# A hybrid decoder layer on one core: the two up-projections as two passes of split products, in place of one pass in full precision

## The reference

```
ga = sigmoid(proj[..., OFF_GATE:OFF_GATE + D_MODEL])
gb = sigmoid(proj[..., OFF_GATE + D_MODEL:N_IN])
m = ga * (o_fox @ w_up_fox) + gb * (o_gdn @ w_up_gdn)     # w_up_*: 1024 x 2048
x = x + m @ w_out                                         # w_out: 2048 x 2048
```

## Time and profile before

| | us |
|---|---|
| runs | 3332.43, 3326.76, 3321.94 |
| median | 3326.76 |
| profiled execution, time | 3323.48 |
| profiled execution, span in the trace | 3321.8 |
| mean granted TensorE clock, share of full | 0.942 |

### The profile page before, as it was taken

The page is one execution under the profiler, slowest core; times in us unless marked ns, Lnnn a source line. Parts: engine busy times, 40 slices in busy tenths (PEclk is TensorE's granted clock), DMA queues, the critical chain, the costliest instruction groups (busy, mean ns, idle before and its releaser), DMA issues.

```text
span 3321.8 us, 62255 instructions
## 1 busy us (share of the span) xinstructions
PE 2974.1 (90%) x23103; PEld 2821.5 (85%) x23103; DVE 1966.2 (59%) x3901; ACT 1291.2 (39%) x2225; POOL 187.6 (6%) x203
## 2 busy tenths in 40 slices
PE   6999899787888997706999999999899999999989
PEld 6999689566666897705999999999789999999979
DVE  4467467332332255597666666666766666666654
ACT  4455420032231044303544444444444444444444
POOL 0000110000000000005100000000520000000000
PEclk8999889589899998858999999999999999999999
DMA  5554200267676453200455554455034455455533
GB/s 186 184 182 178 106 1 1 82 254 285 250 287 234 152 190 120 96 0 0 149 181 177 180 185 177 178 184 183 26 136 181 177 180 185 178 178 183 183 143 128
DMA packets 82018, 519.70 MB, mean 156 GB/s; under 512 B 9186, under 2 KB 9458, under 8 KB 28914
## 3 DMA queue, kind: packets, MB, share of 16 engines
q1 hardware_dynamic: 69394, 468.37, 39.0%
q0 software_dynamic: 11360, 45.61, 3.6%
q10 hardware_dynamic: 1152, 4.19, 0.3%
HBM read 508.75 MB, written 9.39 MB: 156 GB/s over the span
## 4 chain that ended last, share of the span: by engine, by line
PE 79%; DMA 7%; DVE 7%; POOL 2%; issue 2%; SPq 2%; POOLq 0%; ACT 0%; DVEq 0%; ACTq 0%
PE ps L563 22%; PE ps L564 22%; PE ps L565 21%; PE ps L943 4%; DMA arena<-in_vx 3%; DMA arena<-in_kx 3%; PE ps L1006 2%; POOL arena L1363 2%; PE ps L744 2%; SPq L477 1%; PE ps L623 1%; DVE arena L1907 1%; PE ps L732 1%; PE ps L558 1%; PE ps L615 1%
## 5 line engine op out<-in xcount | busy, mean ns | idle before, releaser
L563 PE MATMUL ps<-split 128*128 128x264 f32 x6288 | 1807.1, 287 | 52.1 <-DVE split L405 52.1
L564 PE MATMUL ps<-split 128*128 128x264 f32 x6288 | 1797.3, 286 | 0.0
L565 PE MATMUL ps<-split 128*128 128x264 f32 x6288 | 1791.8, 285 | 0.0
L405 DVE TENSOR_TENSOR split<-arena,split 128x512 fp32r<-128x512 f32 x1568 | 1079.8, 691 | 920.9 <-ACT split L400 918.1
L400 ACT ACTIVATE split<-arena 128x512 fp32r<-128x512 f32 x1568 | 987.7, 632 | 1340.1 <-PE ps L565 1339.7
L563 PEld LDWEIGHTS ps<-split 128*128 128x128 f32 x6288 | 1196.6, 190 | 81.9 <-issue 45.6
L564 PEld LDWEIGHTS ps<-split 128*128 128x128 f32 x6288 | 1196.5, 190 | 1.3 <-issue 0.5
L565 PEld LDWEIGHTS ps<-split 128*128 128x128 f32 x6288 | 1191.8, 190 | 0.3
L1952 DVE TENSOR_TENSOR arena<-arena,ps 128x264 f32<-128x264 f32 x512 | 216.5, 423 | 5.9 <-PE ps L565 5.9
L1363 POOL TENSOR_TENSOR arena<-arena 128x512 f32<-128x512 f32 x66 | 121.7, 1844 | 1264.1 <-DVE arena L1907 1264.1
L1006 PE MATMUL ps<-arena 128*128 128x128 f32 x1056 | 136.3, 281 | 40.5 <-POOL arena L1363 40.5
(11 more groups left out here) (302 smaller groups left out, 1572.6 us busy)
## 6 DMA issues: line engine op xcount, KB each, us to landing
arena<-in_wd SPq DMA_DIRECT2D x280, 1024.0 KB, 4.8
arena<-in_vd SPq DMA_DIRECT2D x128, 1024.0 KB, 4.8
arena<-in_kx POOLq DMA_DIRECT2D x32, 512.0 KB, 7.0
arena<-in_kx SPq DMA_DIRECT2D x32, 512.0 KB, 4.3
arena<-in_vx SPq DMA_DIRECT2D x32, 512.0 KB, 3.9
arena<-in_vx POOLq DMA_DIRECT2D x32, 512.0 KB, 7.2
arena<-in_state POOLq DMA_DIRECT2D x8, 512.0 KB, 7.4
o_ss<-arena ACTq DMA_DIRECT2D x8, 512.0 KB, 8.0
```

Source lines behind the costliest of these rows:

```text
L405: nc.vector.tensor_tensor(ckl(q), at(WR + (s % 4) * D_MODEL + q * QW, QW), as_f32(ckh(q)), ALU.subtract).then_inc(lo_ready, 1)
L563: mm(out, wh, xh, start=start, stop=False)
L564: mm(out, wh, xl, start=False, stop=False)
L565: return mm(out, wl, xh, start=False, stop=stop)
```

## The change

The up-projections join the split stream, in two passes of 8 units. A unit now holds the 8 input blocks of one branch for two output blocks. The first pass, `upg`, is the GDN branch, and stands ahead of `sot`; the second, `upf`, the attention branch, behind it. Each pass needs the high and low part of its 8 activation blocks, one copy of 2112 columns on ScalarE (`oh_split`) and one subtraction of 2112 columns on VectorE (`ol_split`) for each. `upg`'s results are multiplied into the gates in place (`gate_gdn`); `upf`'s are multiplied, added to these and split (`merge`). The merged blocks lie in two places (`MH`, `ML`), and `out` reads them there. The ring's slots are now given back by `lo_ready` in every stage; x is loaded again after `upg`, since it waits for `of_ready`.

```diff
-            ("gates0", 16), ("spt", 2), ("spb", 1), ("gates1", 16), ("sot", 1), ("up", 16), ("out", 16),
+            ("gates0", 16), ("spt", 2), ("spb", 1), ("gates1", 16), ("upg", 16), ("sot", 1), ("upf", 16), ("out", 16),
...
+        MH, ML = (HH + 8 * T, AH), (HL + 8 * T, AL)
...
+            def up_pass(name, s0, xh, xl):
+                with pe.Fori(0, 2) as it:
+                    for j in range(RING):
+                        for q in range(RING):
+                            n = JOB[name] + 2 * j + q // 2
+                            if q % 2 == 0:
+                                pe.wait_ge(evac[n % 4], it * 2 + n // 4)
+                            wait_low_part(pe, it, 4, s0 + j, q)
+                            for kk in range(QK):
+                                k = (q % 2) * QK + kk
+                                last = products(bank(n)[:, 0:T], ckh(q)[:, kk * P:(kk + 1) * P], ckl(q)[:, kk * P:(kk + 1) * P],
+                                                xh(k), xl(k), k == 0, k == NH - 1)
+                            last.then_inc(quarter_done, 1)
+
+            pe.wait_ge(ol_split, 1)
+            up_pass("upg", S0["up"], lambda k: sp_(AH + k * T, T), lambda k: sp_(AL + k * T, T))
+
             n = JOB["sot"]
...
-            pe.wait_ge(of_ready, 1)
-            with pe.Fori(0, 4) as it:
-                for j in range(RING):
-                    n = JOB["up"] + j
-                    pe.wait_ge(w_loaded[j], it * 16 + 16 * (S0["up"] // 4 + 1))
-                    pe.wait_ge(evac[n % 4], it + n // 4)
-                    for half in range(2):
-                        for k in range(NH):
-                            last = mm(ps[:, n % 4 + 4 * half, 0:T], wr(j)[:, (half * NH + k) * P:(half * NH + k + 1) * P],
-                                      ot3[:, half * NH + k, :], start=(k == 0), stop=(k == NH - 1))
-                    last.then_inc(pe_job, 1)
+            pe.wait_ge(ol_split, 2)
+            up_pass("upf", S0["up"] + 8, lambda k: hh3[:, k, :], lambda k: hl3[:, k, :])
             pe.wait_ge(mt_ready, 1)
...
+            act.wait_ge(bn_ready, 40)
+            A(sp_(AH, NH * T), at(OT + NH * T, NH * T), ACT.Copy).then_inc(oh_split, 1)
+            dense_steps(act, S0["up"], 2, high_part, lambda it, j: None, True, False)
+            act.wait_ge(of_ready, 1)
+            A(sp_(HH, NH * T), at(OT, NH * T), ACT.Copy).then_inc(oh_split, 1)
...
+            dense_steps(act, S0["up"] + 8, 2, high_part, merged_high, False)
...
+            dve.wait_ge(oh_split, 1)
+            V.tensor_tensor(sp_(AL, NH * T), at(OT + NH * T, NH * T), as_f32(sp_(AH, NH * T)), ALU.subtract).then_inc(ol_split, 1)
...
+            def merge(it, j):
+                for i in range(2):
+                    n, b = JOB["upf"] + 2 * j + i, 2 * j + i
+                    wait_quarter(dve, it, 4, S0["up"] + 8 + j, 2 * i + 1)
+                    m, t = at(TMU + i * 2 * T, T), at(TMU + (i * 2 + 1) * T, T)
+                    V.tensor_tensor(t, up_block(GT, it, b), bank(n)[:, 0:T], ALU.mult).then_inc(evac[n % 4], 1)
+                    dve.wait_ge(evac[n % 4], it * 2 + (n // 4 + 1))
+                    V.tensor_tensor(m, t, up_block(GT + 16 * T, it, b), ALU.add).then_inc(merged, 1)
+                for i in range(2):
+                    b = 2 * j + i
+                    dve.wait_ge(merged, it * 8 + (b + 1))
+                    dve.wait_ge(mh_ready, it * 8 + (b + 1))
+                    V.tensor_tensor(merged_part(ML, it, b), at(TMU + i * 2 * T, T), as_f32(merged_part(MH, it, b)),
+                                    ALU.subtract).then_inc(mg_step, 1)
```

More of the change, by code:

```diff
@@ L65 @@
 JOB = {}
-SPLIT_JOBS = ("A", "gates0", "gates1", "out", "wq", "u0", "u1", "ple")
+SPLIT_JOBS = ("A", "gates0", "gates1", "upg", "upf", "out", "wq", "u0", "u1", "ple")
 PJ = []
@@ L77, in split_index @@
 def split_index(s):
-    return s if s < S0["up"] else s - 16
+    return s
 def stream_of(n):
@@ L386, in wait_slot @@
         def wait_slot(eng, it, m, s, back=0):
[L388 to L391, removed]
+            eng.wait_ge(lo_ready, it * (4 * m) + 4 * (split_index(s) + 1 - back))
         def high_part(act, it, m, s, q):
@@ L424, in dense_steps, with merged_part @@
                 step(its - 1, j, final and j == RING - 1)
+        def merged_part(base, it, b):
+            if isinstance(it, int):
+                return sp_(base[it] + b * T, T)
+            return split[:, bass.ds(it * (base[1] - base[0]) + (base[0] + b * T), T)]
         def load_pages(eng, part, s, odd, some=range(PAGES)):
@@ L1223, in _, with merged_high @@
             each_block("gates1", 4, ACT.Sigmoid, GT, S0["gates"] + 16, 16)
[L1225 to L1228, removed]
+            act.wait_ge(bn_ready, 40)
[3 more added lines that the diff above has]
+            A(sp_(HH, NH * T), at(OT, NH * T), ACT.Copy).then_inc(oh_split, 1)
+            def merged_high(it, j):
+                for i in range(2):
+                    act.wait_ge(merged, it * 8 + (2 * j + i + 1))
+                    A(merged_part(MH, it, 2 * j + i), at(TMU + i * 2 * T, T), ACT.Copy).then_inc(mh_ready, 1)
+            dense_steps(act, S0["up"] + 8, 2, high_part, merged_high, False)
             def high_only(name):
@@ L1758, in _, with up_block, gate_gdn @@
                                 AX.X, ALU.add).then_inc(on_ready, 1)
+            dve.wait_ge(oh_split, 1)
+            V.tensor_tensor(sp_(AL, NH * T), at(OT + NH * T, NH * T), as_f32(sp_(AH, NH * T)), ALU.subtract).then_inc(ol_split, 1)
+            wait_evac(dve, JOB["gates1"] + 15)
+            def up_block(base, it, b):
+                return at(base + (it * 8 + b) * T, T) if isinstance(it, int) else arena[:, bass.ds(it * (8 * T) + (base + b * T), T)]
+            def gate_gdn(it, j):
+                for i in range(2):
+                    n = JOB["upg"] + 2 * j + i
+                    wait_quarter(dve, it, 4, S0["up"] + j, 2 * i + 1)
+                    gb = up_block(GT + 16 * T, it, 2 * j + i)
+                    V.tensor_tensor(gb, gb, bank(n)[:, 0:T], ALU.mult).then_inc(evac[n % 4], 1)
+            dense_steps(dve, S0["up"], 2, low_part, gate_gdn, True, False)
             wait_evac(dve, JOB["spb"])
@@ L1766, in _ @@
             dve.sem_inc(evac[n % 4], 1)
-            wait_evac(dve, JOB["gates1"] + 15)
             dve.wait_ge(of_ready, 1)
[L1771 to L1785, removed]
@@ L1786, in _ @@
-            dve.wait_ge(mg_step, 32)
+            dve.wait_ge(oh_split, 2)
+            V.tensor_tensor(sp_(HL, NH * T), at(OT, NH * T), as_f32(sp_(HH, NH * T)), ALU.subtract).then_inc(ol_split, 1)
+            def merge(it, j):
+                for i in range(2):
+                    n, b = JOB["upf"] + 2 * j + i, 2 * j + i
[4 more added lines that the diff above has]
+                    V.tensor_tensor(m, t, up_block(GT + 16 * T, it, b), ALU.add).then_inc(merged, 1)
+                for i in range(2):
+                    b = 2 * j + i
[3 more added lines that the diff above has]
+                                    ALU.subtract).then_inc(mg_step, 1)
@@ L1787, in _ @@
+            dense_steps(dve, S0["up"] + 8, 2, low_part, merge, False)
+            dve.wait_ge(mg_step, 16)
             dve.sem_inc(mt_ready, 1)
@@ L2006, in cols, with up_units @@
         return c(a.reshape(T, tiles, P).transpose(2, 1, 0)).reshape(P, tiles * T)
-    up = np.concatenate([x["w_up_fox"][0], x["w_up_gdn"][0]], 0)
+    def up_units(w):
+        return w.reshape(NH, P, 8, 2, P).transpose(2, 1, 3, 0, 4).reshape(8, P, D_MODEL)
     wd = np.concatenate([
         blocks(w_in[:, 0:OFF_F]), blocks(w_in[:, OFF_G:OFF_A]), blocks(w_in[:, OFF_Z:OFF_GATE]),
-        blocks(w_in[:, OFF_GATE:]), blocks(up), blocks(x["w_out"][0]), blocks(x["peer_w_q"][0]),
+        blocks(w_in[:, OFF_GATE:]), up_units(x["w_up_gdn"][0]), up_units(x["w_up_fox"][0]), blocks(x["w_out"][0]), blocks(x["peer_w_q"][0]),
         x["peer_u"][0].reshape(N_KEYS, P, KT, P).transpose(0, 3, 2, 1).reshape(N_KEYS, P, D_MODEL),
```

11 lines of the change are left out of this document (6 added, 5 removed).

## The result

The changed kernel takes 3353.35 us (median of four runs, 3348.9 to 3358.6) against 3327.22 of the kernel before: 1.0079 times as long, 95% interval 1.0057 to 1.0101. The forecast was a gain of 12.8 us; it is a loss of 26. The edited stage, which I priced, came out close to its price. The code behind it, which moved with the edit, I had not looked at.

A forecast was written before the change was run, and what follows sets the result against it. PE was taken to bound the up-projections: 92.8 + 4.4 + 7.5 + 3.2 = 107.9 us against 120.6, start 0.1 earlier, so 12.8 us less. Put on the median, the forecast was 3314 us, range 3305 to 3321.

The forecast's parts named there:

- What bounds the kernel: PE bounds the up-projections, not transfers; only its 120.64 us up to `out` change, and later stages keep their waits.
- The rate, 5.80 us a unit: Both up-projection passes: 16 units as split products at the rate of `out`, 92.8 us, 21.6 less than 114.4.
- The start: Ahead of `upg`: copy hidden, subtraction and first low part let PE begin at 1047.7, 0.1 us gained.
- The gap: Between `upg` and `upf`: turn, own term, copy and subtraction uncovered, 7.5 us, bounds 6.5 to 9.5.
- The clock: Low clock behind the start of each pass: 2.4 us for `upg`, 2.0 for `upf`, sum 4.4, bounds 0 and 6.6.
- The seam to `out`: From the end of `upf` to the first product of `out`: 3.2 us against 3.5 before, 0.3 gained.
- Merge loop hidden: In `upf`: DVE's low parts and merges take 5.3 of 5.80 us a unit, slack 0.8, costed at nothing.
- The rival of a starved pass: Passes starved in part, or a dearer gap: 5.6 us lost to merges, 3319.6, or 3318.2; chance 0.20.
- Sum of the change itself: From up-projections to `out`: 107.9 us against 120.6, start 0.1 earlier, 12.8 us less.
- the one on the slower side: `upf` paced by its merge loop: 3 us more a unit, 24 us lost against 12.8 won, 3338; chance 0.05.
- the gain is given back: Behind `out`: something that doesn't move with PE, only x loaded later found, takes the time up again, 3327; chance 0.05.

The follow-up runs named there:

- the run with 256: The kernel before with 256 more satisfied waits on TensorE, exactly one block, at an idle place: 3326.95 us, 1.0000 of the kernel before.
- the version that fills it: Changed kernel with turn, own term, copy and subtraction moved among units of `upg`, 84 padding instructions: 3308.41 us; repeated, 3297.14 us.
- the run with 204: The changed kernel with 204 more satisfied waits on TensorE at an idle place ahead of the PEER mixer: 3315.79 us, 0.9965 of the kernel before.
- seven kernels: The kernel before, alone and with 36 or 256 idle waits added; the changed kernel, alone and with 204, 110 or 64: 3315.79 to 3411.42 us.
- the two further versions: Changed kernel, padded, with the gap between passes closed: 3308.41 and 3297.14 us; the same with the GDN blocks also split earlier: 3297.05 and 3298.92 us.
- the runs with 64 and 256: 64 more satisfied waits on TensorE in the changed kernel: 3411.42 us, 1.0243; 256 more in the kernel before: 3326.95 us, 1.0000.
- the last version: Changed kernel, padded, gap between passes closed, with the GDN blocks also split earlier, beside gates1: 3297.05 us, 0.9926; repeated, 3298.92 us, 0.9916.

## Why the prediction was wrong, step by step

- **What bounds the kernel: the step that failed.** I took it that "only what PE does between 1047.80 and 1168.44" changes, and that "`norm`, `wq` and the PEER mixer keep their waits". With that the sum had nothing for all that lies behind `out`. The PEER mixer did not keep its waits: its semaphores came as before, but its code had moved, and six stalls on instruction fetches came with it, 36 us with their low clock. TensorE's code ahead of the second PEER loop grew by 548 instructions as I counted when I chose the 36 (547 in the compiled programs), two blocks of 256 and 36 more. The two whole blocks cost nothing, as the run with 256 shows for one; the 36 put the loop over eight blocks in place of seven. The same 36 on the kernel before cost 35 us.
- **The rate, 5.80 us a unit: right.** Read-outs in `upg` run from 1062.90 to 1103.50, seven units, 5.80 each; in `upf` seven read-outs that stand behind low parts run from 1118.22 to 1153.03, 5.80 each again. The estimate of 112.5 ns from one warm matmul to the next, by the rule of the Trainium skill ("TensorE: Matmul & The Clock Gate", section "Wait — 56ns, not 53.3ns?"), does not hold for these products; 120.8 does, again.
- **The start: right.** 4.7 us from the end of the last page product to the first product, against 5.0 before, 0.3 gained where 0.1 was summed.
- **The gap: right.** From the turn's start at 1102.03 to PE's next product at 1109.45 it is 7.4 us; 7.5 was summed. It need not be paid: the version that fills it takes 6.4 to 7.6 us less in this stretch.
- **The clock: a little dear.** `upg` took 48.4 us with 46.4 of work, `upf` 48.0; 3.6 us in both, 4.4 summed. In the run with 204 the whole stretch took 1.1 us more with the same code, so this difference is within the scatter.
- **The seam to `out`: right.** 3.0 us, 3.2 summed: 92.8 + 3.6 + 7.4 + 3.0 = 106.8.
- **Merge loop hidden: right.** No wait on a low part appears inside `upf`. The rival of a starved pass did not come about.
- **Sum of the change itself:** in the stretch 13.8 by the profile of the changed kernel and 12.7 by that of the run with 204; 11.5 by the time of the run with 204; 12.8 forecast.
- **The rivals:** the one on the slower side was another mechanism than the one that came, and "the gain is given back" (0.05) looked for data that comes late, not for code. The profile of before held what was needed for a warning, though not the sum: the fetch queue with 74 packets, and two loops of 6.4 packets each. That the second stood at most 0.14 of a block short of the loss could be seen only by counting instructions in both programs.

Two pages of the Trainium skill state the parts of it. "Advanced Engine Details and Errata", section "ISA Cache", gives TensorE 128 KB in lines of 16 KB, 256 instructions, which would be eight lines; the runs agree with this, as far as they go, if one of the eight is fetched ahead. The "Only 2 cache lines!" of the same list they contradict. "Runtime: NRT & Kernel Launch", section "Instruction fetch mechanics", says that a taken branch whose target is not held must wait for its page. The stalls of 4.4 us fit this: two fetches lie in the one looked at, and none is made in a turn of a held loop. The same section says that what is held is a window of two pages; here a loop of 6.4 was taken back six times with 9 fetches in 690 us, so for TensorE that is not so.

Left open: how far ahead a fetch is made and exactly which instruction sets it off. The rule of seven or eight touched blocks fits all fourteen loop places of seven kernels, and the two further versions, but only with a constant added to my count, which the runs bound (0.10 to 0.25 of a block) and do not explain. The constant was fitted to six of these kernels; the runs with 64 and 256 and the last version were then as the rule said. Counted in the compiled programs, labels left out, the rule needs a constant as well, 36 to 71 instructions. Why some loops stall twice each time round and others once is not settled either.

## What to carry to other kernels

A change to a long unrolled engine program moves all the code behind it. Before and after such a change, look at the instruction queue's packets on the page: if they grow by more than the code did, a loop that was held is being read anew, and "issue" waits at its return, with a low clock behind each, are the price. Then shift it with idle instructions where the engine waits anyway. A loop of at most six blocks would touch no more than seven wherever it stands, and so be held by the rule found here; no run tries this. And judge an edit only against a version whose loops stand as well as those of before.

## What was not expected of the hardware

- 36 instructions that do nothing cost 35 us, 256 of them nothing, and 204 won 37.6.
- A loop of 1639 instructions was held by TensorE and read once in 690 us; moved by 0.14 of a block it was read nine packets each time.
- The longest stalls on a fetch are 2.8 to 5.2 us by kernel and line (means 2.6 to 4.5), and behind them PE works at 1.2 GHz for a while, as it did behind the waits of the earlier trace rows.
- Runs of one program lie up to 24 us apart (3283.51 and 3307.94). In the profiles here the last key-page product starts between 848.3 and 866.8, in code that is the same, while the last 2228 us agreed within 2 in the four profiles compared. Two programs were profiled twice. Their spans differ by 11.6 and 13.0 us, and the starts of that product by 13.6 and 10.1; that the scatter of every program lies there is likely, and not shown.
